# The third expert's gate and up products of the first group, taken apart on TensorE

## The reference, cut to what matters

```python
# 32 experts in 4 groups of 8; each token goes to the best 2 experts of its best group
# w_gate, w_up: (32, 1024, 512) f32, w_down: (32, 512, 1024) f32
def run_block(args):
    xb, e = args
    return (jax.nn.silu(xb @ w_gate[e]) * (xb @ w_up[e])) @ w_down[e]
```

## Time and profile before

| what | value |
| --- | --- |
| median of 3 runs | 968.81 us (968.12 to 970.31) |
| time of the profiled execution | 968.45 us |
| its span, first to last instruction | 966.7 us |
| mean granted TensorE clock | 0.909 of full |
| busy share of the span: TensorE, VectorE, ScalarE, GpSimd | 82%, 49%, 33%, 10% |
| moved by DMA | 286.97 MB, mean 297 GB/s |

### The profile page before, as it was taken

One profiled execution on the slowest core, in us unless ns is written; L12 is line 12 of the kernel. 1 busy time (PEld: TensorE's weight loads), 2 busy tenths in 40 slices (PEclk: granted clock), 3 DMA queues, 4 the chain that ended last, 5 costly groups with the idle time before them and its releaser, 6 DMA issues.

```text
span 966.7 us, 15912 instructions
## 1 busy us (share of the span) xinstructions
PE 795.3 (82%) x6624; PEld 604.3 (63%) x6624; DVE 475.1 (49%) x837; ACT 318.5 (33%) x518; POOL 95.5 (10%) x114
## 2 busy tenths in 40 slices
PE   8999999999867673756747576468898999999997
PEld 6989999787525341333423334236877888888885
DVE  5855848655313220312203122035848687766766
ACT  5764346633100000000000000004585454444444
POOL 2029564300000000000000000000100000000000
PEclk9999999999978887778867788689999999999999
DMA  9984244578999999999999999999955356555101
GB/s 314 300 318 175 96 166 174 213 283 348 426 426 428 426 427 428 424 429 424 426 430 424 428 425 428 427 425 361 361 179 175 115 186 201 201 190 174 44 1 44
DMA packets 72296, 286.97 MB, mean 297 GB/s; under 512 B 11610, under 2 KB 38432, under 8 KB 59680
## 3 DMA queue, kind: packets, MB, share of 16 engines
q1 hardware_dynamic: 71620, 284.81, 74.7%
q10 hardware_dynamic: 604, 1.10, 0.3%
HBM read 284.85 MB, written 1.05 MB: 296 GB/s over the span
## 4 chain that ended last, share of the span: by engine, by line
PE 51%; DMA 31%; SPq 5%; issue 4%; POOL 3%; ACT 3%; DVE 2%; POOLq 0%; DVEq 0%; ACTq 0%
DMA down_a<-in_w_down_dram 30%; PE bank L639 12%; PE bank L588 9%; PE bank L604 9%; PE bank L2268 5%; PE bank L601 4%; SPq L852 4%; PE bank L2249 2%; PE bank L616 2%; DMA lru_w<-in_lru_wi_dram 1%; PE bank L2024 1%; ACT w_hi L558 1%; PE bank L2215 1%; PE bank L2236 1%; PE bank L2223 1%
## 5 line engine op out<-in xcount | busy, mean ns | idle before, releaser
L568 DVE TENSOR_TENSOR w_lo<-ring,w_hi 128x1024 fp32r<-128x1024 f32 x135 | 173.6, 1286 | 107.8 <-ACT w_hi L558 107.3
L558 ACT ACTIVATE w_hi<-ring 128x1024 fp32r<-128x1024 f32 x136 | 144.2, 1061 | 185.7 <-PE bank L604 64.0
L588 PE MATMUL bank<-act_p,w_hi 128*128 128x256 f32 x736 | 138.2, 289 | 3.2 <-issue 1.7
L1746 DVE COPY y_e<-bank 32x256 f32<-32x256 f32 x64 | 27.1, 424 | 225.3 <-PE bank L2268 224.9
L588 PEld LDWEIGHTS bank<-act_p,w_hi 128*128 128x128 f32 x736 | 115.9, 193 | 5.7 <-issue 3.3
L604 PE MATMUL bank<-act_p,w_hi 128*128 128x512 f32 x344 | 119.1, 397 | 0.0
L1195 ACT ACTIVATE y_e<-bank 32x256 f32<-32x256 f32 x64 | 23.9, 373 | 269.7 <-PE bank L2268 269.3
L588 PE MATMUL bank<-act_p,w_lo 128*128 128x256 f32 x368 | 104.7, 284 | 0.0
L2268 PE MATMUL bank<-down_a,h_t 128*32 128x256 f32 x512 | 45.5, 517 | 65.3 <-DMA down_a<-in_w_down_dram 55.7
L2249 PE MATMUL bank<-ring,x_t 128*32 128x256 f32 x1408 | 88.5, 403 | 8.8 <-issue 8.8
L639 PE MATMUL bank<-w_hi,act_q 128*128 128x512 f32 x288 | 91.5, 399 | 3.8 <-issue 3.3
(11 more groups left out here) (408 smaller groups left out, 1079.5 us busy)
## 6 DMA issues: line engine op xcount, KB each, us to landing
ring<-in_w_up_dram SPq DMA_DIRECT2D x24, 2048.0 KB, 34.6
ring<-in_w_gate_dram SPq DMA_DIRECT2D x23, 2048.0 KB, 30.2
down_a<-in_w_down_dram SPq DMA_DIRECT2D x16, 2048.0 KB, 25.8
down_b<-in_w_down_dram SPq DMA_DIRECT2D x15, 2048.0 KB, 26.2
ring<-in_w_in_dram SPq DMA_DIRECT2D x14, 2048.0 KB, 17.5
ring<-in_w_ffn_in_dram SPq DMA_DIRECT2D x22, 1024.0 KB, 7.6
pair_d<-in_w_gate_dram SPq DMA_DIRECT2D x8, 2048.0 KB, 30.3
pair_d<-in_w_up_dram SPq DMA_DIRECT2D x8, 2048.0 KB, 34.8
```

The costliest lines, as they stand in the source:

```text
L558: nc.scalar.activation(parts(w_hi, g, view), view, ACT.Copy).then_inc(split_hi, 1)
L568: engine.tensor_tensor(parts(w_lo, g, view), view, h, ALU.subtract).then_inc(split_lo, 1)
L588: mm = nc.tensor.matmul(dst, parts(wt, g, grans[g][1])[:, k, :], a[:, x_part, k, :], start=(k == 0 and i == 0), stop=(k == KC - 1 and i == 2))
L1746: ins = nc.vector.tensor_copy(y_e[CAP * e:CAP * (e + 1), 256 * j:256 * (j + 1)], bank[2][CAP * j:CAP * (j + 1), 0:256])
```

## The change

The third expert of the first group (expert 2) is multiplied with `gate_up_apart` in place of `gate_up_pe`, and SyncE asks for the gate half that goes into its buffer (expert 6's) behind `gate_read` 4, so behind expert 2's gate product, and no longer behind `gu_raw` 3, the end of both. The up half of expert 6 keeps its wait for `gu_raw` 3. All other waits, the order of the loads, and the experts from 3 on stay as they are.

```diff
@@ -708,6 +708,7 @@
     LOGIT_BANK = (6, 1)
     LAST_DOWN = 2
+    APART = 3
@@ -804,13 +805,13 @@
         sp.wait_ge(gu_raw, 1)
         load_half(0, 1, 4)
         for i in range(1, 4):
-            if i == 1:
-                sp.wait_ge(gate_read, 3)
+            if i < APART:
+                sp.wait_ge(gate_read, i + 2)
+                load_half(i, 0, 4 + i)
+                sp.wait_ge(gu_raw, i + 1)
             else:
                 sp.wait_ge(gu_raw, i + 1)
-            load_half(i, 0, 4 + i)
-            if i == 1:
-                sp.wait_ge(gu_raw, 2)
+                load_half(i, 0, 4 + i)
             load_half(i, 1, 4 + i)
             sp.wait_ge(ye_raw, i)
             load_down(i - 1, i + 1)
@@ -2321,7 +2322,10 @@
             down_pe(4 * k, 0, 2 * k + 1, before is None)
-            gate_up_pe(k, s, 2)
+            if before is None:
+                gate_up_apart(2)
+            else:
+                gate_up_pe(k, s, 2)
             pe.wait_ge(h_ready, 4 * k + 2)
             gate_up_pe(k, s, 3)
```

## The result

The changed kernel takes 963.60 us (median of 4 runs, 962.42 to 963.96), the kernel before 968.99 us on the same chip. The ratio is 0.9941, with a 95% interval of 0.9924 to 0.9958, so it is faster by 0.4 to 0.8%. The forecast was 968.9 us, no change, in a range of 966.9 to 970.9: it was wrong. In later runs beside the experiments the changed kernel came to 964.17 us (ratio 0.9952, 0.9938 to 0.9967). The profiled execution took 962.42 us, its span is 960.7 us.

A forecast was written before the change was run, and what follows sets the result against it. The prediction took the full DMA queue in the stage of the experts as the bound. 968.45 us profiled + 0 (TensorE) + 0 (request) + 0.1 (code) gave 968.55, as a median 968.9 us, no change, range 966.9 to 970.9.

The forecast's parts named there:

- TensorE's products: Expert 2's product in 128 records instead of 64: +0.06 us, hidden by idle time before its down product, so 0.
- The down product of expert 1: Late by 0.06 us on TensorE, as is the request behind it; hidden by loads landing ahead, so 0.
- The request: Expert 6's gate half asked for 1.69 us earlier, at 247.19 us; only waits longer in the queue, worth 0.
- The queue as the bound: In the stage of the experts, bytes, rate and when the DMA queue filled set the end, not single products or requests.
- The term for code: Longer TensorE program shifts the loop's code; fetches delay loads on a DMA engine: +0.1 us, bounds -3.2 and +3.2.
- rival B: Loop of the experts: the code shift makes two present lag steps fall on other engines, 966.7 us, chance 0.07.
- the rule that the prediction names: From the Trainium skill: code comes in 256-instruction blocks, and a taken branch to code outside the window forces a fetch.
- The price: Code fetches in the stage of the experts: 4.6 us of landing lag in all for 32 fetches.
- The sum: Profiled 968.45 us plus 0 for TensorE, 0 for the request, 0.1 for code: 968.55, or 968.9 as median.

The follow-up runs named there:

- e1: Changed kernel with expert 6's gate half asked for behind gu_raw 3 again, as before; TensorE as changed: 964.53 us, ratio 0.9954 to the kernel before.
- e9: Changed kernel with both halves of expert 6 asked for later, behind the second down product: 964.10 us, beside 964.17 for the changed kernel.
- e5: Kernel before with 128 instructions more of straight code in the second group (8 chunks in two calls each): 965.68 us, ratio 0.9966.
- e8: Kernel before with 384 instructions more of straight code in the second group (24 chunks in two calls each): 966.27 us, ratio 0.9977.
- e10: Changed kernel with three idle products on TensorE at some 740 us, behind the loop: 962.90 us, ratio 0.9939 to the kernel before.
- e2: Changed kernel with expert 3 of the first group also multiplied in halves, 128 instructions more of straight code: 969.17 us, ratio 1.0008 to the kernel before.
- e4: Changed kernel with one expert per loop pass in 64 calls, loop body 128 instructions longer: 968.96 us, ratio 0.9999 to the kernel before.
- e11: Kernel before with three idle products on TensorE at some 740 us, behind the loop: 968.17 us, ratio 0.9992.
- e12: Changed kernel run again unaltered, beside other runs on one chip: 964.17 us (963.14 to 966.37).
- e6: Kernel before with 96 instructions more of straight code in the second group (6 chunks in two calls each): 964.80 us, ratio 0.9953.
- e7: Kernel before with 160 instructions more of straight code in the second group (10 chunks in two calls each): 967.68 us, ratio 0.9982.
- e3: Changed kernel with expert 3 of the first group and expert 0 of the second also in halves, 384 instructions above the kernel before: 966.76 us, ratio 0.9975.

## Why the prediction was wrong

*TensorE's products: right in the price, 0, with one miss.* Expert 2 took 3.75 us (3.70 forecast), its down product was hidden as before. The down product of expert 1 was forecast 0.06 us late; in the changed kernel TensorE paused after its first 2 of 32 matmuls (0.47 us idle), and the request behind it came 9.74 us after that for `down_a` instead of 8.64. Those 1.1 us are hidden by the loads ahead, as the forecast said of the 0.06.

*The request: right.* 1.71 us earlier (1.69 forecast), 19.0 us to landing (18.9 forecast), worth nothing; e1 and e9 show it.

*The queue as the bound: right*, and it is why the rest is so clear. In every trace without fetches in the two passes and at full clock in the first product (the changed kernel twice, e1, e5, e8, e9, e10) it is 421.3 to 421.6 us from the first request to the last whole load. With fetches in both passes (the kernel before, e2, e4, e11) it is 424.5 to 425.0.

*The term for code: here it failed.* It was put at +0.1 us, "half a fetch more", with bounds of 3.2 us each way and a chance of 0.07 for the good side (rival B, 966.7 us). The mechanism was the right one: a fetch takes about 1.07 us of a DMA engine, and the slowest of a load's 16 parts sets its landing. That the time of a fetch falls on one engine was inferred, and fits the first parts that keep their time. What was wrong is the number of fetches: I let the shift add or take away one in each pass. It takes away all: 18 in two passes, none left. That a body of code runs from what is kept, or is fetched as a whole, was not weighed, though the rows could have asked the question: 9 packets of 16 KB in 120 us, about one pass, are enough for the whole body of 1750 instructions, fetched anew in a loop that repeats itself. The Trainium skill, "Runtime: NRT & Kernel Launch", section "Instruction fetch mechanics", gives TensorE room for 2048 instructions, more than this body has. It also has the rule that the prediction names, that a taken branch to code outside a window of two pages forces a fetch. The kernel before agrees, with 9 fetches a pass. In the changed kernel the branch back over the same 1750 instructions forced none, and there the measurement decides against the rule. The price was a little low as well: at 4.6 us of lag for 32 fetches, 17 fewer would give back 2.4 us, and 3.3 to 3.4 came back. That the good side was in the prediction at all, as rival B with 966.7 us, was no foresight: B had two steps fall on other engines, not the fetches gone.

*Behind the stage: not foreseen, half explained.* The sum let the gain or loss end with the stage. From the last whole load to the last small load of `lru_w` it is 41.2 us before and 39.9 after, and from there to the end 267.7 and 267.0. The second goes with the clock spell, which the kernel before's trace has and the changed kernel's has not; e12, the changed kernel with a spell, has 268.0. So this part can come and go with the execution. The first is 39.9 to 41.0 us where the code behind the loop lies 128 or 129 instructions further than in the kernel before (the changed kernel twice, e1, e5, e9, e10), 40.9 and 41.0 with 96 and 160 (e6, e7), and 41.2 to 41.7 with none, 256 or 384 (the kernel before, e11, e2, e4, e3, e8). So it seems to go with the place of the code as well, though 41.0 and 41.2 are close, and it is a part of why e3 and e8, whose loops fetch nothing in the two passes, get back only half of the gain. What is late in it I did not find.

## What to carry to other kernels

Where a queue of loads is the bound, whatever else uses the same DMA engines can cost more than its share of them, code fetches included: 18 fetches of 1.07 us are 1.2 us of 16 engines' time, and cost 3.3. So count the instruction packets pass by pass before an edit that changes the length of the code ahead of a loop or in it. Ask for the same loads earlier only where the queue runs dry; here a request could come 7.9 us later at no cost. A gain of half a per cent from such an edit must be tested with the same number of instructions put elsewhere, as it may belong to the place of the code and be lost with the next edit.

## What the runs showed of the hardware that was not expected

A loop of 1750 TensorE instructions ran its second and third pass without a fetch when 128 or 129 instructions more (six traces; 96, one trace, and 384, two, did the same) stood ahead of it than in the kernel before, and with 9 fetches a pass with 0 and 256, or when its body was 1878 long (one place tried); with 160 one pass of two fetched. 9 fetches of 16 KB in each of two passes delayed a stream of 2 MB loads by about 3.3 us, and only by its slow parts: in the 12 traces with full clock in the first product the first part of the last whole load was in 417.7 to 418.0 us after the first request, with fetches or without. TensorE's first product of the stage, at half clock, took 5.37 us instead of 3.70, in the traces of e3 and e6 only, with nothing changed ahead of it.
